# Long convolution: the alternating row first, the last forward group one inverse part earlier, gated rows and gates in pairs

## The reference, cut to what matters

```python
def fft_long_conv(u, spec):
    L = u.shape[1]
    U = jnp.fft.rfft(u.astype(jnp.float32), n=2 * L, axis=1)
    return jnp.fft.irfft(U * spec, n=2 * L, axis=1)[:, :L].astype(u.dtype)

def hyena_seq(t, w_in, conv_w, conv_b, spec, bias, w_out):
    u, gate = jnp.split(t @ w_in, [(HY_ORDER + 1) * HY_WIDTH], axis=-1)
    u = depthwise_conv(u, conv_w, conv_b)
    v, *gates = jnp.split(u, HY_ORDER + 1, axis=-1)
    z = v
    for o in range(HY_ORDER):
        z = gates[o] * (fft_long_conv(z, spec[:, o]) + z * bias[o])
    return (z * jax.nn.silu(gate)) @ w_out
```

## Time and profile before

| | |
|---|---|
| median of 3 runs | 2025.62 us (2024.8 to 2028.76) |
| the profiled execution's own time | 2025.27 us |
| its span, first to last instruction | 2023.4 us |
| mean granted TensorE clock | 0.991 |
| the stage `hyena` | from about 1636 us to the end |

### The profile page before, as it was taken

How to read it: one execution, slowest core, us unless ns; L and a number is a source line. 1 busy time by engine, 2 the same in 40 slices (tenths; PEclk the granted TensorE clock), 3 DMA queues, 4 the chain that set the end, 5 groups by cost and what they waited for, 6 DMA issues and landing times.

```text
span 2023.4 us, 24604 instructions
## 1 busy us (share of the span) xinstructions
PE 1963.8 (97%) x9830; PEld 1645.7 (81%) x9830; DVE 1372.6 (68%) x1954; ACT 828.8 (41%) x1307; POOL 231.7 (11%) x234
## 2 busy tenths in 40 slices
PE   8999999999999999999999999999999999999997
PEld 6888887788888888888888888778888878888786
DVE  5477766997798667756754874555555567787774
ACT  5233334542233345544332443444344444544442
POOL 2133221003211320010000001100000101001011
PEclk9999999999999999999999999999999989999998
DMA  5211123336444431123444332311111323332331
GB/s 183 74 58 62 53 63 103 132 129 220 166 151 146 151 110 42 32 79 140 156 146 141 139 115 94 104 63 42 42 34 40 116 75 122 94 136 80 139 94 53
DMA packets 60963, 208.40 MB, mean 103 GB/s; under 512 B 6832, under 2 KB 7152, under 8 KB 59696
## 3 DMA queue, kind: packets, MB, share of 16 engines
q1 hardware_dynamic: 53296, 193.19, 28.6%
q10 hardware_dynamic: 7552, 13.64, 1.9%
HBM read 196.31 MB, written 10.49 MB: 102 GB/s over the span
## 4 chain that ended last, share of the span: by engine, by line
PE 79%; DVE 12%; ACT 5%; issue 3%; POOL 1%; DMA 0%; ACTq 0%; DVEq 0%; SPq 0%
PE PS L324 20%; PE PS L328 20%; PE PS L327 20%; PE PS L436 3%; DVE wlo L1881 2%; PE PS L935 2%; PE PS L331 1%; PE PS L334 1%; PE PS L335 1%; ACT whi L1198 1%; PE PS L924 1%; PE PS L687 1%; PE PS L728 1%; DVE col_f L2102 1%; PE PS L544 1%
## 5 line engine op out<-in xcount | busy, mean ns | idle before, releaser
L324 PE MATMUL PS<-nhi,whi 128*128 128x512 f32 x1456 | 589.6, 405 | 15.5 <-DVE wlo L1881 3.4
L328 PE MATMUL PS<-nhi,wlo 128*128 128x512 f32 x1456 | 571.3, 392 | 0.0
L327 PE MATMUL PS<-nlo,whi 128*128 128x512 f32 x1456 | 570.4, 392 | 0.0
L1881 DVE TENSOR_TENSOR wlo<-raw,whi 128x1024 fp32r<-128x1024 f32 x291 | 368.5, 1276 | 176.2 <-ACT whi L1198 175.1
L1198 ACT ACTIVATE whi<-raw 128x1024 fp32r<-128x1024 f32 x291 | 303.5, 1053 | 207.4 <-PE PS L324 132.9
L324 PEld LDWEIGHTS PS<-nhi,whi 128*128 128x128 f32 x1456 | 275.9, 189 | 77.6 <-issue 9.7
L328 PEld LDWEIGHTS PS<-nhi,wlo 128*128 128x128 f32 x1456 | 275.1, 189 | 59.7
L327 PEld LDWEIGHTS PS<-nlo,whi 128*128 128x128 f32 x1456 | 275.9, 190 | 51.9 <-issue 1.0
L2731 POOL TENSOR_TENSOR diag<-diag,sqb 128x512 f32<-128x512 f32 (+1 forms) x56 | 73.6, 1314 | 778.2 <-ACT sqb L1207 695.7
L324 PE MATMUL PS<-hh_f,whi 128*128 128x512 f32 x352 | 137.2, 390 | 0.0
L328 PE MATMUL PS<-hh_f,wlo 128*128 128x512 f32 x352 | 137.0, 389 | 0.0
(11 more groups left out here) (358 smaller groups left out, 3366.7 us busy)
## 6 DMA issues: line engine op xcount, KB each, us to landing
raw<-in_stream SPq DMA_DIRECT2D x291, 512.0 KB, 3.5
aw_f<-in_ada SPq DMA_DIRECT2D x48, 512.0 KB, 4.4
rows<-sd_f ACTq DMA_DIRECT2D x32, 256.0 KB, 2.3
rows_h<-rows SPq DMA_DIRECT2D x8, 1024.0 KB, 6.1
wd_f<-in_decay ACTq DMA_DIRECT2D x16, 256.0 KB, 3.0
hT<-in_xT SPq DMA_DIRECT2D x8, 256.0 KB, 7.5
out<-hT SPq DMA_DIRECT2D x8, 256.0 KB, 2.0
wd_f<-in_filt_out ACTq DMA_DIRECT2D x8, 128.0 KB, 3.1
```

Source lines behind the costliest of these rows:

```text
L324: op = e.matmul(out, hi, xh, start=first, stop=False)
L327: e.matmul(out, hi, xl, start=False, stop=False)
L328: return e.matmul(out, lo, xh, start=False, stop=last)
L1881: e.tensor_tensor(m.wlo[:, c % HL, :], m.raw[:, c % RAW, :], m.whi[:, c % HL, :].bitcast(F), SUB).then_inc(*s.w_lo.tick(c))
```

## The change

Three orders change; no matmul, copy or product is added or left out.

In the first forward group the two tiles `alt` come first and go to bank `bu` in place of `bk`; ACT reads them first, then `bk`, writes row 0's `hm` behind that, and then reads `bj`. `bu`'s own matmuls wait until ACT has read the alternating row. DVE does its part of `hm` after four tiles in place of ten.

The sequence of a convolution becomes f0 f1 i0 f2 f3 i1 i2 i3 (it was f0 f1 i0 f2 i1 f3 i2 i3), on PE, ACT and DVE.

In part 2 the projections stand as two gated rows, two gates, two gated rows, two gates (they stood in turn).

```diff
+CONVOLVE = [("forward", 0), ("forward", 1), ("inverse", 0), ("forward", 2), ("forward", 3), ("inverse", 1), ("inverse", 2),
+            ("inverse", 3)]
+GATED = [(0, 0), (0, 1), (1, 0), (1, 1), (0, 2), (0, 3), (1, 2), (1, 3)]
...
-            for ct in range(4):
+            for gate, ct in GATED if part == 2 else [(0, ct) for ct in range(4)]:
...
             def forward(j):
                 sums, differences = (0, 1), (2, 3)
+                if j == 0:
+                    for k, x in enumerate(sums):
+                        w = tiles.take([("alt", k, 0)])
+                        if k == 0:
+                            q.wait_ge(*(s.taken_v.at("bu", *prev, 3) if prev else s.h.at("mla_out", 1)))
+                            q.wait_ge(*s.made_v.at("h_lo", od, c, 0))
+                        op = mm_w(bu, w, a.hh[:, 0, x, :], a.hl[:, 0, x, :], k == 0, k == 1)
+                    op.then_inc(*s.filled.tick("alt", od, c))
...
-                        q.wait_ge(*(s.taken_v.at("bu", *prev, 3) if prev else s.h.at("mla_out", 1)))
+                        q.wait_ge(*s.taken_a.at("alt", od, c))
                     op = mm_w(bu, w, a.zh[:, k, :], a.zl[:, k, :], k == 0, k == 1)
...
-            forward(0)
-            for j in range(1, 4):
-                forward(j)
-                if j == 3 and (od, c) != (1, 1):
+            for step, j in CONVOLVE:
+                if step == "forward":
+                    forward(j)
+                else:
+                    inverse(j)
+                if (step, j) == ("forward", 3) and (od, c) != (1, 1):
                     for x in range(2):
                         tiles.mark(("rows", *((0, 1) if od else (1, c)), x), x)
-                inverse(j - 1)
-            inverse(3)
...
             def forward(j):
                 i = j % 2
+                if j == 0:
+                    for _ in range(2):
+                        w.tiles(1)
+                    q.wait_ge(*s.filled.at("alt", od, c))
+                    if od:
+                        q.wait_ge(*s.made_v.at("hg", c, 3))
+                    elif c:
+                        q.wait_ge(*s.made_v.at("inv", 1, 0, 3))
+                    e.activation(a.alt[:, :], bu, ACT.Copy).then_inc(*s.taken_a.tick("alt", od, c))
...
-                e.activation(ks[:, 0, :], bk, ACT.Copy).then_inc(*s.taken_a.tick(*key))
+                e.activation(ks[:, 0, :], bk, ACT.Copy).then_inc(*s.taken_a.tick("bk", od, c, j))
+                if j == 0:
+                    q.wait_ge(*s.made_v.at("row 0", od, c))
+                    e.activation(a.hh[0:1, 0, 0, :], a.hm[0:1, :], ACT.Copy).then_inc(*s.made_a.tick("hm", od, c))
...
-                for _ in range(10 if j == 0 else 8):
-                    w.tiles(1)
                 if j == 0:
+                    for _ in range(4):
+                        w.tiles(1)
                     q.wait_ge(*s.made_a.at("hm", od, c))
                     e.tensor_tensor(a.hl[0:1, 0, 0, :], a.hm[0:1, :], a.hh[0:1, 0, 0, :].bitcast(F),
                                     SUB).then_inc(*s.made_v.tick("hm", od, c))
+                for _ in range(6 if j == 0 else 8):
+                    w.tiles(1)
```

More of the change, by code:

```diff
@@ L1005, in free, with free2 @@
                         q.wait_ge(*s.taken_v.at("inv", *((0, c) if part else (1, 0)), ct))
[L1006 to L1012, removed]
+                def free2():
+                    if ct > 1:
+                        q.wait_ge(*s.taken_v.at("hg", c, ct - 2))
+                    else:
+                        q.wait_ge(*s.taken_v.at("inv", 0, c, 2 + ct))
+                if gate:
                     yield from project(2 + ct % 2, "hy_in", 24 + 4 * c + ct, ("hyg", c, ct), nhi, nlo, free2)
+                else:
+                    yield from project(ct % 2 if part == 2 else ct, "hy_in", col, ("hy", col), nhi, nlo, free, ready5)
         def filters(od, c):
@@ L1080, in forward @@
                 op.then_inc(*s.filled.tick("bj", od, c, j))
[L1081 to L1087, removed]
                 for k in range(2):
@@ L1753, in channels @@
                 return
-            for ct in range(4):
+            for gate, ct in GATED if part == 2 else [(0, ct) for ct in range(4)]:
                 col = 8 * part + 4 * c + ct
                 yield from w.steps(KD)
-                conv(col, ct, c, part)
-                if part == 2:
-                    yield from w.steps(KD)
+                if not gate:
+                    conv(col, ct, c, part)
+                else:
                     q.wait_ge(*s.filled.at("hyg", c, ct))
@@ L1794, in forward @@
                     q.wait_ge(*s.sums.at("n5"))
-                key = ("bk", od, c, j) if j else ("bk", od, c, 0, "first")
-                e.activation(ks[:, 0, :], bk, ACT.Copy).then_inc(*s.taken_a.tick(*key))
+                e.activation(ks[:, 0, :], bk, ACT.Copy).then_inc(*s.taken_a.tick("bk", od, c, j))
+                if j == 0:
+                    q.wait_ge(*s.made_v.at("row 0", od, c))
+                    e.activation(a.hh[0:1, 0, 0, :], a.hm[0:1, :], ACT.Copy).then_inc(*s.made_a.tick("hm", od, c))
                 for _ in range(2):
@@ L1800, in forward @@
                 e.activation(ks[:, 1, :], bj, ACT.Copy).then_inc(*s.taken_a.tick("bj", od, c, j))
-                if j == 0:
-                    for _ in range(2):
-                        w.tiles(1)
[L1804 to L1811, removed]
                 for _ in range(4):
@@ L2580, in channels @@
                 return
-            for ct in range(4):
+            for gate, ct in GATED if part == 2 else [(0, ct) for ct in range(4)]:
                 col = 8 * part + 4 * c + ct
                 yield from w.steps(KD)
-                conv(col, ct, g[:, ct, :] if part else z[:, ct, :])
-                if part == 2:
-                    yield from w.steps(KD)
+                if not gate:
+                    conv(col, ct, g[:, ct, :] if part else z[:, ct, :])
+                else:
                     q.wait_ge(*s.made_a.at("hg", c, ct))
@@ L2620, in forward @@
                                     SUB).then_inc(*s.made_v.tick("hm", od, c))
+                for _ in range(6 if j == 0 else 8):
+                    w.tiles(1)
                 q.wait_ge(*s.filled.at("bu", od, c, j))
-                q.wait_ge(*s.taken_a.at(*(("bk", od, c, j) if j else ("bk", od, c, 0, "first"))))
+                q.wait_ge(*s.taken_a.at("bk", od, c, j))
                 if j:
@@ L2630, in forward @@
                 kx = ks[:, 0, :] if j else a.alt[:, :]
-                q.wait_ge(*s.taken_a.at("bk", od, c, j))
+                if j == 0:
+                    q.wait_ge(*s.taken_a.at("alt", od, c))
                 e.tensor_tensor(tmp[:, 3, :], bi, kx, MUL).then_inc(*s.taken_v.tick("bi", od, c, j))
```

## The result

| | before | after |
|---|---|---|
| median of 4 runs each | 2025.21 us (2023.9 to 2028.76) | 2015.41 us (2014.43 to 2015.87) |
| ratio, 95% interval | | 0.9948 [0.9931, 0.9965] |
| the profiled execution | 2025.27 us | 2015.16 us |
| its span | 2023.4 us | 2013.3 us |

Five further runs of the changed kernel gave 2017.49 us and a ratio of 0.9965 [0.9952, 0.9978], so two sets of runs of one program lie 2 us apart. What follows is therefore read inside the stage, from the start of C1's first matmul to the start of the program's last: 340.22 us before and 331.27 after, 331.24 in the profile of the five.

The account below looks back on a forecast made before the run. PE, busy 97% of the span, bounds the kernel. Gains of 3.1, 0.85, 0.8 and 2.6 us in the four convolutions make 7.3, so 2025.27 becomes 2018.0, 2018.2 us for a median; range 2015.2 to 2022.0.

Parts of the forecast that it names:

- the fall: Behind the second half's 2.1 us wait for weights: PE's clock at 0.54 on average, 1.7 us lost, kept in the sum.
- The rival that held this: Behind the weights' wait the clock doesn't fall: 1.7 us more gained, 2016.3 us; chance 0.13.
- Edits 1 and 2: Alternating row first, and fourth forward group ahead of second inverse part: together all 7.3 us of the forecast gain.
- the 9.0 us: Whole sum if the clock's fall behind the weights' wait is absent after the change: 9.0 us in place of 7.3.
- Edit 1: Alternating row first: PE's waits for `hl_h` go in the first and fourth convolutions, 1.68 + 1.61 = 3.3 us.
- Edit 2: Fourth forward group ahead of second inverse part: last inverse part's waits for `y_lo` fall from 4.3 to about 0.8 us.
- its rival (given back): ACT's and DVE's chain is slower than walked, last inverse part waits as now: only 3.3 us gained, 2022.0; chance 0.13.
- C2 and C3: Second and third convolutions: last inverse part's waits for `y_lo` shrink from 0.94 and 0.84 us; gains 0.85 and 0.8.
- f3's wait for `bu`: Fourth convolution, last forward group: PE waits some 0.1 us for bank `bu`.
- Edit 3: Gated rows and gates in pairs: no listed PE wait is touched; 0 us, bounds of +-0.2.
- SP's queue: First and second convolutions: one weight chunk more queues behind the rows' DMA; cost nothing, or a microsecond for each one late.
- The likeliest case: Forecast without rivals, each of three chains 0.4 us off: 2016.8 to 2019.6 us; chance 0.60.

Follow-up runs that it names:

- the shifted kernels: Spare matmuls ahead of the weights' wait: 9 or 18 in the changed kernel (297.39, 297.86 us to the last `nlo` wait), 9 in the kernel before (stage 340.71 us).
- DVE's place alone: Against the kernel before, only DVE's `hl_h` subtraction moved, to after six tiles in place of ten: 2024.68 us, ratio 0.9992.
- edit 2 alone: Against the kernel before, only the sequence of a convolution changed, to f0 f1 i0 f2 f3 i1 i2 i3: 2020.57 us, ratio 0.9971.

## Why the prediction was right about the stalls and wrong about the clock

**The step that failed** is the last one of the working: "The change leaves that stall as it is, so I keep the fall in the sum." The stall did stay (2.25 us after, 2.23 before), and the fall did not: 1.6 us, the whole difference of the stage to the forecast. The rival that held this (2016.3 us, chance 0.13) is what happened; its 1.7 us measured 1.6. What it argued against itself, that the stall stays, is no argument, as the shifted kernels show: the same wait with the same matmuls around it has the fall or not by when it comes. Edits 1 and 2 had put it 4.9 us earlier in the stage, and the working should have asked where that lands. Nor was this fall the only one of the stage, as the prediction has it: the last two matmuls of the kernel before come at 0.51. Of the 2.8 us between 2018.2 and 2015.41, the fall behind the weights' wait is 1.6; nearly all the rest is the 1.1 us ahead of the stage, which no edit made.
The Trainium skill (TensorE: Matmul & The Clock Gate, Part 1: The HAM clock gate) has the monitor's window run freely, not tied to the kernel's start. The shifted kernels agree that one stall may be followed by the fall or not, and the 9.0 us that the prediction works out by that rule stand beside 8.95. But near moments agree in the outcome, also in two profiles of one kernel whose C1 begins 3.3 us apart; free running alone would leave that to chance.

**Edit 1** was right step by step. In the frame of the kernel before (1.13 us later) ACT reads bk at 1676.58, the predicted figure, `hl_h` is done at 1678.47 (said: 1678.4), and p0 comes 1.19 us earlier (1.12). ACT's and DVE's timelines after, against the earlier trace rows:

```profile
1674.09 0.60 ACT L1800 ACTIVATE rb<-PS 128x512 f32<-128x512 f32 x1
1675.45 0.60 ACT L1810 ACTIVATE sqb<-PS 128x512 f32<-128x512 f32 x1 [0.76 <-PE PS L331]
1675.95 0.61 ACT L1813 ACTIVATE hh_h<-rb 1x512 fp32r<-1x512 f32 x1
...
1676.66 0.68 DVE L2625 TENSOR_TENSOR hl_h<-rb,hh_h 1x512 fp32r<-1x512 f32 x1 [1.09 <-ACT hh_h L1813]
1678.39 1.23 DVE L1887 TENSOR_TENSOR wlo<-raw,whi 128x1024 fp32r<-128x1024 f32 x1 [1.05 <-ACT whi L1204]
1679.53 0.68 DVE L2633 TENSOR_TENSOR tmp_h<-PS,sqb 128x512 f32<-128x512 f32 x1
```

PE's order was not what mattered for the wait itself: DVE's place alone removes both. The rest of edit 1 brings `whi` forward, which is worth something only where i3 waits for the chain, in C4 (2.20 against 2.63 us).

**Edit 2** was right too, its rival (given back) wrong. In C1 `y_hi`(3) stands behind i1's end, as said, at 1701.68, which is 1702.81 in the frame before; said was 1702.61, and i3 has no wait. C2 and C3 were sized to 0.05 us (they keep 0.19 and 0.09, where under 0.1 was said of each). In C4 the chain goes as walked:

```profile
1942.39 1.19 ACT L1824 ACTIVATE yh<-tmp_h 128x512 fp32r<-128x512 f32 x2 [3.37 <-POOL tmp_h L2799]
1943.49 0.62 ACT L1851 ACTIVATE nhi<-o_h 128x512 fp32r<-128x512 f32 x1
1944.01 0.58 ACT L1810 ACTIVATE sqb<-PS 128x512 f32<-128x512 f32 x1
1944.49 1.04 ACT L1204 ACTIVATE whi<-raw 128x1024 fp32r<-128x1024 f32 x1
```

`whi` follows `y_hi`(2) by 2.10 us, as predicted. Counted back by the 7.56 us gained until there (1.13 + 3.26 + 0.81 + 0.76 + 1.6), `y_hi`(2) lies at 1949.95 (said: 1949.96) and i3 at 1958.37 (1958.35). Mis-sized were two small terms: f3's wait for `bu`, 0.1 said and 0.22 measured, and with it i3's own wait, 0.49 in place of 0.7.

**Edit 3 and SP's queue** cost nothing, as said: no wait for a bank or a transfer has joined PE's list.

**The rest**, 1.1 us, lies ahead of the stage, where no instruction changed.

**The sums.** The first two rivals are counted from the profiled execution, and the forecast for a median, 0.35 us later: 2016.3 and 2022.0 are 2016.5 and 2022.3 for a median. The likeliest case, 2018.2 with three chains 0.4 us off, spans 2017.0 to 2019.4. None of this changes the step that failed.

## What to carry to other kernels

Walk the chain of the engine that is late, split by split, in the frame of the old trace: here it gave 7.3 us of stalls to within 0.1. A fall of the clock behind a stall is not a property of that stall; when an edit ahead of it shifts it by microseconds, price the fall as a chance and not as kept. Before reordering PE, try the late engine's own place in its queue: one moved subtraction removed both waits for `hl_h`, though 0.9 us came back at C4's i3.

## What the runs showed of the hardware

- A weights' wait of 2.2 us is followed by half clock or not by its moment, with the same work around it: five profiles with, seven without, 1.6 us each, and a shift of 2.05 us turns it either way. The program's last two matmuls too come at half clock or not (0.51 before, 0.94 with edit 2 alone), 0.5 us. What ties the outcome to the place in the stage was not measured.
- Ahead of the stage one program's executions differ: C1 begins at 1672.53 and at 1675.81 us in two profiles of the same kernel. Differences of whole runs under some 3 us are read better inside the stage.
